# Seven of the first expert's weight chunks are loaded behind the stores of the normed rows and of x

## The reference

```python
logits = hf @ w_router + b_router            # 512 tokens, 32 experts
top_v, top_i = lax.top_k(logits, 4)
top_w = softmax(top_v)
# for each token and each of its 4 experts e:
gu = h @ w_gate_up[e] + b_gate_up[e]         # [1024] -> [2048]
gate, up = minimum(gu[:1024], 7), clip(gu[1024:], -7, 7)
y += top_w * (((up + 1) * gate * sigmoid(1.702 * gate)) @ w_down[e] + b_down[e])
```

## Time and profile before

| | |
|---|---|
| median of 3 runs | 2091.08 us (2089.45 to 2095.82) |
| the profiled execution, its own time | 2085.34 us |
| its span in the trace | 2083.6 us |
| granted TensorE clock over the span | 0.999 |
| busy share of the span: PE, PEld, DVE, ACT, POOL | 99%, 60%, 41%, 22%, 18% |
| DMA moved | 520.14 MB, mean 250 GB/s |
| loads of expert weights | 256 gate/up and 128 down, 1024 KB each; median 20.9 and 22.6 us to landing |

### The profile page before, as it was taken

One profiled execution on the slowest core, in us unless ns is written; L12 is line 12 of the kernel. 1 busy time (PEld: TensorE's weight loads), 2 busy tenths in 40 slices (PEclk: granted clock), 3 DMA queues, 4 the chain that ended last, 5 costly groups with the idle time before them and its releaser, 6 DMA issues.

```text
span 2083.6 us, 42388 instructions
## 1 busy us (share of the span) xinstructions
PE 2054.8 (99%) x17798; PEld 1246.7 (60%) x17798; DVE 862.4 (41%) x1468; ACT 455.5 (22%) x741; POOL 369.3 (18%) x413
## 2 busy tenths in 40 slices
PE   9999999999999999999999999999999999999999
PEld 6888876344443444443443443447786788888887
DVE  4554435433333333332333332324665443444544
ACT  5151442000000000000000000024554532212211
POOL 2010001112222222222223223221202400000000
PEclk9999999999999999999999999999999999999999
DMA  7334126999999999999999999974111022323221
GB/s 263 101 122 131 61 81 254 385 400 406 408 414 407 408 413 409 408 413 406 396 412 408 408 412 404 410 257 135 61 61 41 1 81 70 112 81 101 86 102 54
DMA packets 141117, 520.14 MB, mean 250 GB/s; under 512 B 16460, under 2 KB 71936, under 8 KB 91808
## 3 DMA queue, kind: packets, MB, share of 16 engines
q1 hardware_dynamic: 120384, 495.02, 60.2%
q0 software_dynamic: 20672, 24.26, 5.0%
HBM read 509.09 MB, written 18.88 MB: 253 GB/s over the span
## 4 chain that ended last, share of the span: by engine, by line
PE 88%; DMA 7%; DVE 2%; ACT 2%; issue 1%; SPq 0%; POOL 0%; POOLq 0%; DVEq 0%; ACTq 0%
PE ps L2246 27%; PE ps L2260 13%; PE ps L395 12%; PE ps L397 12%; PE ps L396 12%; DMA ring<-in_w_gate_up 4%; DMA ring<-in_w_down 3%; PE ps L2054 1%; PE ps L2111 1%; PE ps L2141 1%; PE ps L497 1%; PE ps L1882 1%; PE ps L1903 1%; PE ps L2048 1%; PE ps L2004 1%; PE ps L2074 1%
## 5 line engine op out<-in xcount | busy, mean ns | idle before, releaser
L2246 PE MATMUL ps<-ring,xe 128*32 128x512 f32 x6144 | 668.7, 592 | 1.3 <-DMA ring<-in_w_gate_up 1.2
L2246 PEld LDWEIGHTS ps<-ring,xe 128*32 128x32 f32 x6144 | 197.1, 110 | 428.8 <-issue 405.0
L2260 PE MATMUL ps<-ring,act_t 128*32 128x256 f32 x6144 | 338.8, 379 | 3.2 <-DMA ring<-in_w_down 1.9
L2260 PEld LDWEIGHTS ps<-ring,act_t 128*32 128x32 f32 x6144 | 200.9, 110 | 148.7 <-issue 17.1
L395 PE MATMUL ps<-xt_hi,hi 128*128 128x512 f32 x544 | 213.6, 393 | 0.8 <-DVE ff_a L1734 0.8
L397 PE MATMUL ps<-xt_hi,lo 128*128 128x512 f32 x544 | 211.8, 389 | 0.0
L396 PE MATMUL ps<-xt_lo,hi 128*128 128x512 f32 x544 | 211.7, 389 | 0.0
L1139 ACT ACTIVATE glu<-glu 128x768 f32<-128x768 f32 x32 | 27.0, 844 | 635.3 <-DVE glu L1687 635.3
L789 POOL DMA_INDIRECT x_rows<-ye,idx x96 | 152.9, 1593 | 37.6 <-issue 37.6
L1654 DVE COPY idx<-idx 128x3 int32<-128x3 int32 x33 | 5.6, 169 | 352.6 <-DMA x_rows<-ye,idx 345.5
L382 DVE TENSOR_TENSOR lo<-raw,hi 128x2048 fp32r<-128x2048 f32 x44 | 101.3, 2309 | 92.2 <-ACT hi L375 85.3
(11 more groups left out here) (339 smaller groups left out, 2464.8 us busy)
## 6 DMA issues: line engine op xcount, KB each, us to landing
ring<-in_w_gate_up SPq DMA_DIRECT2D x256, 1024.0 KB, 20.9
ring<-in_w_down SPq DMA_DIRECT2D x128, 1024.0 KB, 22.6
raw<-in_w_in SPq DMA_DIRECT2D x20, 1024.0 KB, 6.3
raw<-in_w_gate SPq DMA_DIRECT2D x11, 1024.0 KB, 5.3
raw<-in_w_up SPq DMA_DIRECT2D x11, 1024.0 KB, 5.3
raw<-in_w_down SPq DMA_DIRECT2D x11, 1024.0 KB, 4.9
raw<-in_w_out SPq DMA_DIRECT2D x8, 1024.0 KB, 5.1
raw<-in_w_k SPq DMA_DIRECT2D x4, 1024.0 KB, 5.0
```

What stands on the lines that cost most here:

```text
L2246: last = pe.matmul(ps[QUAD * j:QUAD * j + QUAD, g, :], xe[:, g, QUAD * k:QUAD * k + QUAD], w[:, j, :, :], start=k == 0, stop=k == KT - 1)
L2260: last = pe.matmul(y_block(g, j, bank), act_t[:, g, QUAD * (2 * c + h):QUAD * (2 * c + h) + QUAD], w[:, h, QF * j:QF * j + QF], start=c == ...
```

## The change

The loads of chunks 0 to 6 of expert 0, with their waits on `lo_ready` and `group_done`, are taken out of `sync_program`; the loop in `moe_loads` that loaded chunks 7 and 8 of expert 0 now loads chunks 0 to 8. The slots, the sources, the 16 chunks that are loaded before the main loop, the kept chunks and the loop itself are the same.

```diff
@@ sync_program
             for c in range(1, SA.n):
                 load_chunk(sp, SA, c)
 
-            for q in range(RAW):
-                sp.wait_ge(SA.lo_ready, SA.n - 2 + q)
-                moe_load(sp, 0, q, q)
-            for q in range(3, 7):
-                sp.wait_ge(SA.group_done, SA.first[SA.n - 2 + (q - 3) // 2])
-                moe_load(sp, 0, q, q)
             for t in range(T):
                 sp.wait_ge(n_h, NS["ffn"] + t + 1)
@@ moe_loads
             sp.wait_ge(SA.group_done, SA.first[SA.n])
-            for q in range(7, 9):
+            for q in range(9):
                 moe_load(sp, q // KT, q % KT, q)
             sp.wait_ge(r_lgT, T)
```

## The result

The changed kernel takes 2097.62 us (median of 16 runs, 2094.66 to 2102.66); the kernel before, run as often on the same chip, 2093.38 (2089.45 to 2095.87). The ratio, each time to the kernel before on the same chip, is 1.0024, interval 1.0016 to 1.0032: **5.0 us slower (3.3 to 6.7)**, where +12.9 was forecast. Two repeats gave 1.0036 (1.0022 to 1.0050) and 1.0026 (1.0017 to 1.0035), +7.5 and +5.4 us. So the change costs 5 to 7 us: the sign was right, the size less than half to somewhat over half of the forecast. It lies about at the 6 us that the prediction named as what one measurement can tell from no change; the intervals exclude 0.

The account below looks back on a forecast made before the run. The prediction took DMA time in the MoE, covered by a stock of landed chunks, as the bound. Seven chunks +17.9 less holes 5.0 gave +12.9 us, on the median 2091.08 so 2104 us; range 2097 to 2111.

Parts of the forecast that it names:

- The stock and where it is lost: MoE: landed chunks cover DMA's 32.5 us per expert against TensorE's 31.24; gone near 620 us instead of 900.
- Rival 1: MoE start: the preload was more than enough and TensorE never waits; 0 us, 2091; 7 in 100.
- Rival 2: First expert's gather waits behind the queued loads, so TensorE starts late; +17.9 us, 2109; 6 in 100.
- Rival 3: MoE loads: a deeper queue moves more, 426 GB/s on, so today's waits go; -6 us, 2085; 4 in 100.
- seven chunks: Moved loads ahead of the MoE's unbroken DMA work: 7 x 2.56 us of DMA time, +17.9 us.
- The holes: Idle DMA time early in the MoE, 380 to 465 us, that the moved loads fill: -5.0 us.
- SP's issue and the stores: Group at 351.58: 16 load issues instead of nine, behind the stores; cost nothing, 0.5 us either way for contention.
- The ceiling: MoE ring: a load that takes longer than 28.6 us to land is waited for.
- the same step on the median: Whole kernel: the profiled execution's +12.9 us (2085.34 to 2098.2) added to the median 2091.08, giving 2104.
- Over 28 before 650: MoE loads in the profile after: landings were to exceed 28 us before 650 us.
- About eight experts of 31.24: MoE behind 998 us in the profile after: about eight experts were to take 31.24 us each.
- I am wrong if the shift is under 8: Profile after: a shift under 8 us would mean DMA had more idle time than counted.

Follow-up runs that it names:

- run 5: Kernel before, preload kept, plus seven 1 MB copies into scratch DRAM behind x's stores: 2100.41 us, ratio 1.0038.
- run 4: One extra 512 KB copy per expert into scratch DRAM, in both kernels: before 2116.63 us (1.0129), after 2138.5 us (1.0228).
- run 3: Down loads halved to 512 KB in both kernels: before 2090.2 us (0.9998), after 2089.74 us (1.0001).
- repeat 1: Kernel before, unchanged, run again for a second trace: 2093.52 us, ratio 1.0003.
- repeat 2: Kernel before, unchanged, run again for a third trace: 2094.88 us, ratio 1.0005.
- run 2: Only chunks 3 to 6 moved behind the stores, chunks 0 to 2 left early, against the kernel before: 2093.86 us, 1.0006.

## Why the prediction was right and wrong

**The stock and where it is lost: right.** Landings near 415 us were to be 20 and are 18.3 to 20.0 on the mean of the loads issued from 405 to 420; rates of 405 or more from 380 us on are there; the first expert starts as before; the loss lies ahead of the kept chunks, in experts of 31.8 to 32.8 us, most of them between 720 or 750 us and the kept chunks, and the rest is equal. Rival 1 (0 us) falls by the interval; but for four chunks it is true. Rival 2 falls: expert 0 starts at 375.2 to 379.8 in either kernel (a gather can be held up, but run 5 did it with other copies). Rival 3 falls: the rate is 417 to 418 only in the first 53 us, and 410 again from 496 us on.

**The terms: nearly right.** 17.9 us for seven chunks stands (run 4: 18.9 against 19.4). The holes were put at 5.0 and are a little larger. They were counted against 410 GB/s, and the kernel after moves 417 to 418 in the first two windows; and the repeats of before have deeper holes in them, the first repeat in the first two rows, the second in the last two:

```profile
380.00:402.15 22.15, 22.15 (x198) 6.93 (x194) 5.21 (x12) 3.90 (x7) 3.20 (x4) 1.00 0.99 372
402.15:433.40 31.25, 31.25 (x404) 13.14 (x396) 11.82 (x29) 2.10 (x5) 3.21 (x4) 1.00 0.94 372
...
380.00:402.15 22.15, 22.15 (x210) 6.62 (x203) 1.46 (x8) 2.40 (x4) 3.22 (x4) 1.00 0.91 357
402.15:433.40 31.25, 31.25 (x362) 12.44 (x364) 14.17 (x30) 2.35 (x4) 3.22 (x4) 1.00 0.95 366
```

From 433 to 465 us they move 408 and 406, the kernel after 407. So what the change fills is 5.9 us of DMA time beside the first repeat, 7.3 beside the second and 5.8 beside the first trace. SP's issue and the stores cost nothing that shows (run 3). The ceiling was 28.6 by the sum, and the mean of all loads at it is 28.7.

**The step that failed: "the same step on the median".** The sum took TensorE's pace, 31.24, and with it landings that grow by 1.24 per expert and a stock that is used up by 998 us, from one profiled execution. It saw that this execution lay 5.7 us under the median, and moved the result up by that much, as if it were a shifted copy of an ordinary run. It was not: in an ordinary run of before an expert takes 31.6, the landings grow by 0.90 to 0.96, and 4.7 to 6.3 us of stock are left unused. This rest, which the sum puts at nothing, pays for part of the change:

```
                            repeat 1   repeat 2
seven chunks                  17.9       17.9
less holes that they fill     -5.9       -7.3
less stock left unused        -6.3       -4.7
cost of the change             5.7        5.9      (measured, experts 0 to 19: 5.7)
```

This account was made after the result; run 2 (four chunks cost nothing, and their landings end 1.5 us under the ceiling), run 3 (nothing is short, no cost) and run 4 (nothing is left, 18.9) bear it out. Set against the forecast, experts 0 to 19 are off on both sides:

```
                       before     after    difference
as predicted            620.5     633.2      +12.7
ordinary runs           624.8     630.5       +5.7
off by                   +4.3      -2.7       -7.0
```

The 4.3 are the slower TensorE, which lengthens the kernel before. That the kernel after is 2.7 shorter than forecast is explained in part only: 0.8 are holes, the rest is open. That TensorE's pace lengthens the kernel after less, because an expert takes DMA's 32.4 once the stock is gone, is argued and not shown: no trace has the kernel after with a TensorE at 31.24.

**Luck.** The forecast for the profiled execution after was 2098.2 us and it took 2097.62. That is no proof of the sum: its TensorE ran at 31.54, experts 0 to 19 cost it 8.8 more than the first trace of before and not 12.7, and the other 3.5 us came from a later first expert (379.8 against 377.2) and from behind the MoE.

**The rest.** "Over 28 before 650" was wrong: the loads issued from 640 to 690 us take 25.2 to 27.5 on the mean, those from 740 to 780 us 28.1 to 28.7. "About eight experts of 31.24" behind 998 was wrong: experts 20 to 30 take 31.5 to 31.6 on the mean in all six traces. The mark "I am wrong if the shift is under 8" was set for more idle holes than counted; the shift is under 8 mostly for the other cause, the unused stock.

## What to carry to other kernels

Where loads run ahead of an engine by a stock, write down three numbers per turn (what DMA needs, what the engine needs, how deep the ring lets a load be late) and what is left of the stock at the end: moving DMA work into the busy stretch is free until that rest is used up (here four of seven chunks), and then costs its full DMA time (18.9 us for the seven with no rest). Before an engine's pace is taken from a trace, take a second trace of the same kernel: 1% of pace decided here whether the stock was used up or a fifth of it was left. An execution's own time is a hint to do so and no more; of two that lay below the other runs, one had the quick pace and one did not. Where there is one trace only, work out the sum at a slightly slower pace too, for a difference doesn't carry over to executions that have a margin left.

## What the runs showed of the hardware that was not expected

- The 16 completions of one load drift apart. In the first trace of before, a load issued at 415 us has them after 5.1 us (first), 5.3 (median) and 6.8 (last); one issued at 822, after 10.0, 16.7 and 24.3. The last one sets the landing, so the stock is that of the slowest DMA engine. By the Trainium skill ("DMA: Bandwidth & Descriptors", Why a DMA increments its semaphore by 16 and not by 1) the engines finish independently and only the full 16 means that the data is there; the trace agrees, with these 14 us between the first and the last. What makes one engine the slowest was not tried.
- TensorE runs the same program at 31.24 or about 31.6 us per expert; the slower form comes with a pause of 0.2 to 0.6 us at the second down chunk of most experts and longer weight loads afterwards (0.17 to 0.28 us for four instead of 0.13). One matmul over the whole array between those over 32 columns restores the form of the weight loads, and costs 0.9 us over the 31.24. What the slower form comes from is open.
- An issue on SP was held up to 6.7 us with 16 loads queued, and cost nothing.
- Beside copies from DRAM to DRAM the first expert's gather landed 14.4 us after its issue, against 7.2 in the repeat of before and 6.0 for gathers beside loads into SBUF that take 28. That was one instance.
